# Gate and up products with stationary weights in runs of 16 and 32 of one width, also in the first chunk of three feed-forward parts

## The reference

```python
def swiglu(x, w_gate, w_up, w_down):
    return (jax.nn.silu(x @ w_gate) * (x @ w_up)) @ w_down
# each block:
h = h + 0.5 * swiglu(rms_norm(h, ffn1_norm), ffn1_w_gate, ffn1_w_up, ffn1_w_down)
h = h + mixer(rms_norm(h, mix_norm), ...)      # two attentions, gates, w_out
h = h + 0.5 * swiglu(rms_norm(h, ffn2_norm), ffn2_w_gate, ffn2_w_up, ffn2_w_down)
# the first block ends with one more rms_norm; the second takes its result as x
```

## Time and profile before

| | us |
|---|---|
| median of 3 runs | 1123.94 |
| lowest and highest | 1123.61, 1124.98 |
| span of the profiled execution | 1121.8 |
| PE busy in it | 1115.6 (99%) |
| DVE busy | 782.2 (70%) |
| ACT busy | 627.1 (56%) |

### The profile page before, as it was taken

How to read it: one execution, slowest core, us unless ns; L and a number is a source line. 1 busy time by engine, 2 the same in 40 slices (tenths; PEclk the granted TensorE clock), 3 DMA queues, 4 the chain that set the end, 5 groups by cost and what they waited for, 6 DMA issues and landing times.

```text
span 1121.8 us, 14828 instructions
## 1 busy us (share of the span) xinstructions
PE 1115.6 (99%) x5830; PEld 955.3 (85%) x5830; DVE 782.2 (70%) x1102; ACT 627.1 (56%) x837; POOL 57.8 (5%) x105
## 2 busy tenths in 40 slices
PE   9999999999999999999999999999999999999998
PEld 8888888888888888888888888888888888888887
DVE  6777755765887777775477777456998687777742
ACT  6555532677667456553355655337787864655530
POOL 1000000000000000000000000020353000000000
PEclk9999999999999999999999999999999999999999
DMA  9766565653454566655566655557643455556550
GB/s 319 246 189 190 187 244 190 207 168 131 161 187 160 178 216 189 188 188 188 188 207 188 188 188 188 188 165 255 212 151 116 148 164 176 186 188 189 191 183 37
DMA packets 142581, 208.02 MB, mean 185 GB/s; under 512 B 9296, under 2 KB 100584, under 8 KB 142512
## 3 DMA queue, kind: packets, MB, share of 16 engines
q1 hardware_dynamic: 139408, 198.07, 54.0%
q0 software_dynamic: 3088, 9.00, 2.3%
q10 hardware_dynamic: 16, 0.00, 0.0%
HBM read 205.98 MB, written 2.65 MB: 186 GB/s over the span
## 4 chain that ended last, share of the span: by engine, by line
PE 97%; DVE 1%; ACT 1%; DMA 0%; issue 0%; SPq 0%; DVEq 0%
PE banks L1796 26%; PE banks L1657 16%; PE banks L1659 16%; PE banks L1658 16%; PE banks L1794 14%; PE banks L1975 1%; PE banks L1729 1%; PE banks L1679 1%; PE banks L1949 1%; PE banks L1976 1%; PE banks L1900 1%; DMA raw<-in_ffn_w_gate 0%; PE banks L1933 0%; DVE w_lo L1122 0%; PE banks L1934 0%; PE banks L2040 0%
## 5 line engine op out<-in xcount | busy, mean ns | idle before, releaser
L1122 DVE TENSOR_TENSOR w_lo<-raw,w_hi 128x2048 fp32r<-128x2048 f32 x186 | 422.8, 2276 | 170.3 <-ACT w_hi L739 170.0
L739 ACT ACTIVATE w_hi<-raw 128x2048 fp32r<-128x2048 f32 x186 | 352.5, 1898 | 115.6 <-PE banks L1659 112.0
L1796 PE MATMUL banks<-xT,w_hi 128*128 128x512 f32 x1280 | 313.7, 392 | 0.0
L1796 PEld LDWEIGHTS banks<-xT,w_hi 128*128 128x128 f32 x1280 | 232.8, 189 | 43.2
L1657 PE MATMUL banks<-w_hi,xT 128*128 128x512 f32 (+1 forms) x464 | 183.2, 395 | 0.0
L1659 PE MATMUL banks<-w_hi,xT 128*128 128x512 f32 (+1 forms) x464 | 179.5, 387 | 0.0
L1658 PE MATMUL banks<-w_lo,xT 128*128 128x512 f32 (+1 forms) x464 | 179.2, 386 | 0.0
L1794 PEld LDWEIGHTS banks<-xT,w_lo 128*128 128x128 f32 x1280 | 169.8, 191 | 9.5
L1794 PE MATMUL banks<-xT,w_lo 128*128 128x256 f32 x1280 | 173.5, 283 | 0.0
L1657 PE MATMUL banks<-w_hi,hT_hi 128*128 128x512 f32 x352 | 137.4, 390 | 0.0
L1659 PE MATMUL banks<-w_hi,hT_lo 128*128 128x512 f32 x352 | 137.1, 389 | 0.0
(11 more groups left out here) (293 smaller groups left out, 917.8 us busy)
## 6 DMA issues: line engine op xcount, KB each, us to landing
raw<-in_ffn_w_gate SPq DMA_DIRECT2D x88, 512.0 KB, 4.0
raw<-in_ffn_w_up SPq DMA_DIRECT2D x88, 512.0 KB, 5.0
raw<-in_ffn_w_down SPq DMA_DIRECT2D x88, 512.0 KB, 4.3
raw<-in_w_in SPq DMA_DIRECT2D x76, 512.0 KB, 4.6
raw<-in_w_out SPq DMA_DIRECT2D x16, 512.0 KB, 4.1
raw<-in_w_branch_moba SPq DMA_DIRECT2D x4, 512.0 KB, 4.4
raw<-in_w_branch_sb SPq DMA_DIRECT2D x4, 512.0 KB, 5.6
raw<-in_w_branch_a SPq DMA_DIRECT2D x4, 512.0 KB, 3.8
```

The source lines that it names most:

```text
L739: act.activation(w_hi[u % SLOTS][:, 0:n], raw[u % RAWS][:, 0:n], ACT.Copy).then_inc(hi_done, 1)
L1122: dve.tensor_tensor(w_lo[r][:, 0:n], raw[r][:, 0:n], w_hi[u % SLOTS][:, 0:n], ALU.subtract).then_inc(lo_done, 1)
L1796: m = pe.matmul(bank[b + s], mh, xT[:, k].rearrange("p a s -> p (a s)"), start=k == 0, stop=k == KC - 1)
```

## The change

- In chunks 1 to 10 of all four parts the order becomes: 16 wide and 16 narrow products for hf = 0, then 16 narrow and 16 wide for hf = 1 (`pair_products`, `pair_chunk`, `pair_second`). With the neighbours that makes runs of 32. F0's turned hidden rows and the spread of 1/rms (`spread_rows`) now stand behind the first 16 wide products of chunk 1, before the narrow ones.
- In F1, F2 and F3 the first chunk becomes a pair chunk as well (`first_pairs`), narrow products first. The silu of tokens, its product and the four transposes are left in F0 alone (`first_silu`, `first_hidden`, `turn_hidden`). `spread_rows` stays, and waits for both sums of chunk 0.
- In these parts DVE's scaling of a gate is apart from the sum (`pair_scale`), and that of chunk 0 waits for `rows_copied`.
- Banks: even chunks use 0 to 3, odd ones 4 to 7, w_down sums in 4 to 7 (before 2 to 5), mixers turn x in 0 to 3 (before 0, 1, 6, 7), the spread rows are in bank 3.
- F2 takes its quarters in the order `Q_MIX` (before `Q_FFN`), and F1's w_down units go by it too (`down_quarters`).

```diff
+FIRST = {"F0": 1, "F1": 0, "F2": 0, "F3": 0}
...
         def quarters(ph):
-            return Q_MIX if ph in ("F0", "F1", "F3") else Q_FFN
+            return Q_MIX if ph[0] == "F" else Q_FFN
+
+        def down_quarters(ph):
+            return quarters(NEXT[ph]) if ph in NEXT else Q_FFN
...
-            return bank[2 + 2 * tt + n] if ph[0] == "F" else bank[2 * n + tt]
+            return bank[4 + 2 * tt + n] if ph[0] == "F" else bank[2 * n + tt]
...
-            return (2 if c % 2 else 0) + (2 * p if c % 2 else 6 * p)
+            return 4 * (c % 2) + 2 * p
...
-                silu(ph)
-                split_hi(u0 + 4)
-                hidden_hi(ph)
-                split_hi(u0 + 5)
-                rstd_rows_in(ph)
-                split_hi(u0 + 6)
-                for c in range(1, NCH):
+                if ph == "F0":
+                    act.wait_ge(rstd_done, 1)
+                    first_silu()
+                    split_hi(u0 + 4)
+                    first_hidden_hi()
+                    split_hi(u0 + 5)
+                    rstd_rows_in(ph)
+                    split_hi(u0 + 6)
+                else:
+                    split_hi(u0 + 4)
+                for c in range(FIRST[ph], NCH):
                     low(ph, c, 0)
-                    pair_gate(ph, c, 0)
+                    if c > 0:
+                        pair_gate(ph, c, 0)
                     low(ph, c, 1)
+                    if c == 0:
+                        rstd_rows_in(ph)
+                        pair_gate(ph, c, 0)
...
+            def pair_scale(ph, c, p):
+                n = pairs_before(ph, c) + p
+                if c == FIRST[ph]:
                     dve.wait_ge(rows_copied, FFN_OF[ph] + 1)
...
-                if ph != "F2":
+                if ph == "F0":
                     split_lo(u0 + 3)
-                hidden(ph)
-                split_lo(u0 + 4)
-                hidden_lo(ph)
-                split_lo(u0 + 5)
-                for c in range(1, NCH):
-                    pair_sum(ph, c, 0)
+                    first_hidden()
+                    split_lo(u0 + 4)
+                    first_hidden_lo()
+                    split_lo(u0 + 5)
+                else:
+                    pair_sum(ph, 0, 0)
+                    pair_sum(ph, 0, 1)
+                    if ph != "F2":
+                        split_lo(u0 + 3)
+                for c in range(FIRST[ph], NCH):
+                    if c:
+                        pair_sum(ph, c, 0)
+                    pair_scale(ph, c, 0)
                     pair_hidden(ph, c, 0)
                     split_lo(u0 + 4 + 2 * c)
                     pair_rest(ph, c, 0)
...
+            def pair_chunk(ph, c):
+
+                u = BASE[ph] + 2 * c
                 pe.wait_ge(lo_done, u + 1)
                 for p in range(2):
+                    pair_free(ph, c, p)
+                    pair_products(ph, c, 0, p, False)
+                if c == 1 and ph != "F2":
+                    spread_rows(ph)
+                for p in range(2):
+                    m = pair_products(ph, c, 0, p, True)
                 m.then_inc(unit_used, 1)
+                pair_second(ph, c)
+
+            def pair_second(ph, c):
+
+                pe.wait_ge(lo_done, BASE[ph] + 2 * c + 2)
+                for p in range(2):
+                    pair_products(ph, c, 1, p, True)
+                pair_products(ph, c, 1, 0, False).then_inc(pair_done, 1)
+                if c == 1 and ph == "F2":
+                    spread_rows(ph)
+                pair_products(ph, c, 1, 1, False).then_inc(unit_used, 1)
+
+            def first_pairs(ph):
+
+                u, x0 = BASE[ph], 4 * PREP_OF[ph]
+                turn_x(ph, 2 if ph != "F2" else 1)
+                if ph == "F2":
+                    turn_x(ph, 2)
+                pe.wait_ge(lo_done, u + 1)
+                pe.wait_ge(xT_hi_done, x0 + 2)
+                for p in range(2):
+                    if p:
+                        pe.wait_ge(gained, 4 * (3 if ph == "F2" else GAIN_OF[ph]) + 4)
+                    pair_products(ph, 0, 0, p, True)
+                turn_x(ph, 3)
+                pe.wait_ge(xT_lo_done, x0 + 2)
+                for p in range(2):
+                    m = pair_products(ph, 0, 0, p, False)
...
```

More of the change, by code:

```diff
@@ L1215, in scale_x, with first_hidden, first_hidden_lo @@
                 link(ins)
-            def hidden(ph):
+            def first_hidden():
                 for tt in range(TT):
-                    dve.wait_ge(silu_done, 2 * FFN_OF[ph] + tt + 1)
+                    dve.wait_ge(silu_done, tt + 1)
                     dve.tensor_tensor(hs[tt], bank[tt][:, CH:2 * CH], gsil[tt], ALU.mult).then_inc(h_done, 1)
-            def hidden_lo(ph):
-                dve.wait_ge(hT_hi_done, FFN_OF[ph] + 1)
-                dve.tensor_tensor(hT_lo[:, 0:2, :], bank[6].rearrange("p (k t) -> p k t", k=2),
+            def first_hidden_lo():
+                dve.wait_ge(hT_hi_done, 1)
+                dve.tensor_tensor(hT_lo[:, 0:2, :], bank[2].rearrange("p (k t) -> p k t", k=2),
                                   hT_hi[:, 0:2, :], ALU.subtract).then_inc(hT_lo_done, 1)
@@ L1750, in begin @@
                     return
-                turn_x(ph, EARLY[ph])
+                turn_x(ph, 1)
                 batch(0, 0)
-                for q in range(EARLY[ph] + 1, 4):
+                for q in range(2, 4):
                     turn_x(ph, q)
@@ L1757, in begin @@
                 batch(1, 1)
[L1759 to L1771, removed]
@@ L1773, in pair_chunk, with pair_products @@
-            def pair_chunk(ph, c, hf):
-                f = FFN_OF[ph]
-                u = BASE[ph] + 2 * c + hf
+            def pair_products(ph, c, hf, p, low):
+                u, b = BASE[ph] + 2 * c + hf, pair_banks(c, p)
+                for s in range(2):
+                    for k4 in range(4):
+                        k = 4 * hf + k4
+                        mh, ml = rows(u, NB, k4, s * CH + p * P, P)
+                        first = k == 0 and low == (c == 0)
+                        if low:
+                            m = pe.matmul(bank[b + s][:, 0:SEQ], ml, xT_hi[:, k, :], start=first, stop=False,
+                                          skip_group_check=c == 0)
+                        else:
+                            m = pe.matmul(bank[b + s], mh, xT[:, k].rearrange("p a s -> p (a s)"), start=first,
+                                          stop=k == KC - 1, skip_group_check=c == 0)
+                return m
@@ L1777, in pair_chunk, with pair_free @@
+            def pair_free(ph, c, p):
+                if c >= FIRST[ph] + 2:
+                    pe.wait_ge(pair_summed, pairs_before(ph, c - 2) + p + 1)
+                elif c == 2 and p == 0:
+                    pe.wait_ge(h_done, 2)
+                elif c == 2:
+                    pe.wait_ge(hT_lo_done, 1)
+                if c == 2 and p == 1:
+                    pe.wait_ge(rows_copied, FFN_OF[ph] + 1)
+            def pair_chunk(ph, c):
+                u = BASE[ph] + 2 * c
                 pe.wait_ge(lo_done, u + 1)
@@ L1778, in pair_chunk @@
                 for p in range(2):
[L1779 to L1797, removed]
@@ L1814, in turn_hidden, with spread_rows @@
-                pe.matmul(bank[7][:, 0:SEQ], ones, rstd_diag, start=True, stop=True).then_inc(rows_mm, 1)
+            def spread_rows(ph):
+                if ph == "F0":
+                    turn_hidden()
+                else:
+                    pe.wait_ge(pair_summed, PAIRS[ph] + 2)
+                pe.wait_ge(diag_done, 2 * FFN_OF[ph] + 2)
+                pe.matmul(bank[3][:, 0:SEQ], ones, rstd_diag, start=True, stop=True).then_inc(rows_mm, 1)
             def ffn(ph):
-                begin(ph, lambda tt, hf: first_chunk(ph, tt, hf))
+                if ph == "F0":
+                    begin(ph, None)
+                else:
+                    first_pairs(ph)
@@ L1818, in ffn @@
                 for c in range(1, NCH):
-                    pair_chunk(ph, c, 0)
-                    if c == 1 and ph != "F2":
-                        turn_hidden(ph)
-                    pair_chunk(ph, c, 1)
+                    pair_chunk(ph, c)
                 for d in range(NCH):
@@ L1826, in ffn @@
                     pe.wait_ge(lo_done, u + 1)
+                    if d < FIRST[ph]:
+                        pe.wait_ge(hT_lo_done, 1)
+                    else:
+                        pe.wait_ge(pair_lo, pairs_before(ph, d) + 2)
                     if d == 0:
[L1828 to L1832 removed]
+                        pe.wait_ge(pair_summed, pairs_before(ph, NCH - 1))
+                    for q, (tt, n) in enumerate(down_quarters(ph)):
                         if d == NCH - 1 and q == 3 and ph in NEXT:
```

89 lines of the change are left out of this document (42 added, 47 removed).

## The result

The changed kernel takes 1129.65 us (median of 4 runs, 1128.12 to 1130.16) against 1124.01 us before: a ratio of 1.0049, 95% interval 1.0037 to 1.0061. It is slower, by 5.6 us where 4.2 were forecast. The profiled execution spans 1127.8 us (before 1121.8).

What follows compares the result with a forecast made beforehand. PE's stream of products was taken as the bound. Waits of +6.5 us and work of -2.3 gave +4.2, a profiled 1126.0 and a median of 1128.2 us; the 8-in-10 range was 1126.3 to 1130.7.

Steps and rivals of the forecast that it cites:

- PE's stream is the bound: Whole kernel: PE is busy 1115.6 of 1121.8 us, so work removed is gained and uncovered waits are lost in full.
- Part 1, runs, -1.6: Chunks 1 to 10: two fewer changes of width per chunk at 0.02 us, over 40 chunks, save 1.6 us.
- the prediction's rival: Chunks 1 to 10: changes of width are free, so 1.6 us less is gained, 1129.8 us; chance 0.08.
- Part 2, first chunk and transposes, +0.6 and -1.3: First chunk of F1, F2, F3: 64 products instead of 48 cost 0.6 us; dropped hidden-row transposes save 1.3.
- F0, +1.8: F0, chunk 1: transposes, now ahead of 16 narrow products, wait for DVE's hidden products; 1.8 us lost.
- Seams, +0.7 and +1.6: Starts of F1 and F3: waits for the last quarter's gain, 0.7 us; F2: waits for xT_hi and gain, 1.6.
- F2's chunk 2, +2.4: F2: chunk 2's first unit is split only after the 1/rms chain, so PE waits; 2.4 us lost.
- that rival: F2: PE's clock falls after the 2.4 us wait, costing about 2 us more, 1130.2 us; chance 0.08.
- One sign of being wrong: Listed signs: no idle PE at F2's chunk 2, period 11.15 or under 11.0, or F2 stretches with granted clock under 1.
- The start as evidence for the clock: Kernel start: five 512-column products take 2.50 us, some 0.53 each where 0.23 is usual, read as low pace.
- The thin cover behind it: F2, after chunk 2's wait: next unit split 0.4 us before PE asks, no further wait; further waits up to 1.5 us, chance 0.05.

Runs made afterwards that it cites:

- the runs alone: Kernel before, only the product order of chunks 1 to 10 changed to 16 wide, 16 narrow, 16 narrow, 16 wide: 1122.31 us, ratio 0.9987.
- all waits covered: Changed kernel with F0's transposes later, F2's second quarter turned earlier, gain waits moved or dropped, chunk 2's units in F2 split before the 1/rms wait: 1121.61 us.

## Why the prediction was right, and where its size was off

- **PE's stream is the bound.** Right: F0's wait and the two of F2's seam came back in the time in full when they were taken away, F2's wait at chunk 2 less what a new wait took, and a kernel without any of them is faster than before by the saved work.
- **Part 1, runs, -1.6.** Right: period 11.154 to 11.114, and 1.4 by the runs alone. By the rule of the Trainium skill (TensorE: Matmul & The Clock Gate, "Step-by-step: what each phase is for") that the next weights load while the current product runs, the prediction's rival had 0 here; the measurement decides against 0. It doesn't show what a change of width spends its time on. The prediction took 0.107 us for a load although the trace of before has rows for it, of 0.191 us on average, longer than the 0.12 us from one narrow product to the next. The loads overlap one another (1280 x 0.191 is 244 us, in 169.8 us of busy time; the row has the count, busy us, mean ns and idle us):

```profile
L1794 PEld LDWEIGHTS banks<-xT,w_lo 128*128 128x128 f32 x1280 | 169.8, 191 | 9.5
```

- **Part 2, first chunk and transposes, +0.6 and -1.3.** Right as a sum: -0.7 between the kernel with all waits covered and that with the runs alone. They differ in this and in what goes with it (banks, the order of the quarters, the order of ACT's and DVE's queues), and have the same waits. The two terms were not measured one by one.
- **F0, +1.8.** Right: 1.7 by the rows, 1.7 to 1.8 by the experiment.
- **Seams, +0.7 and +1.6.** F2's was right (1.4 to 1.6). Those of F1 and F3 were not taken away one by one; they are in the 6.6 of all waits. In F1's trace the third quarter's transposes to chunk 1 are 12.40 us against 11.84 in the earlier trace rows, 0.56 more, forecast 0.19 + 0.36; the wait is in the first 16 narrow products, which take 2.37 us instead of some 2.0 (1.91, and 0.09 behind transposes). F3's was not read:

```profile
382.40 0.60 PE L1703 MATMUL banks<-const,xg 128*128 128x128 f32 x4
382.76 2.54 PE L1792 MATMUL banks<-xT,w_lo 128*128 128x256 f32 x16
385.13 0.60 PE L1703 MATMUL banks<-const,xg 128*128 128x128 f32 x4
...
394.80 3.82 PE L1795 MATMUL banks<-xT,w_hi 128*128 128x512 f32 x16
```

- **F2's chunk 2, +2.4.** The wait was right in its place and its length. Its price was not complete: the clock falls behind it in 5 of 9 runs, at 1.6 us. The step of the prediction that failed is the weight given to that rival (0.08, and nothing in the sum) and not its size (2 us). No ground was given for so small a weight: the prediction says itself that waits of up to 1.1 us don't show what a longer one does. The median, 1129.65, is of the rival's group (1130.2 forecast, 1129.8 measured); the forecast's own 1128.2 is the other group's. One sign of being wrong thus came true, a stretch of F2 with a granted clock under 1, and that the median came within 1.5 us of the forecast is in part luck: how many runs of a few have the fall decides it.
- **The start as evidence for the clock.** The prediction read the slow products at the start, 0.53 us each, as a low clock. The granted clock in that stretch was 1.00, so they are no evidence for it, and what slows them stays open:

```profile
1.00:5.00 4.00, 3.94 (x9) 2.50 (x9) 0.31 (x3) 1.01 (x1) 0.00 (x0) 1.00 0.73 207
```

- **The thin cover behind it.** "0.4 us before PE asks for it" held in the changed kernel at full clock: chunk 2's second unit is split by 600.16 and asked for at 600.64. But the two experiments that moved the first unit's split showed this second unit late by 0.3 us.

## What to carry to other kernels

Before the stream of a bound engine is reordered, note for each of its waits what was queued ahead of it as cover: here 16 narrow products ahead of four transposes, and a split ahead of a wait for 1/rms, were worth more than the reordering gained. Where TensorE is the bound, a single idle stretch can cost more than its length, as the one of 2.2 us did in half of the runs here by bringing the lower clock; price it with and without. And move a split or any other long instruction only after following what then stands behind it.

## What the runs showed of the hardware

- A change of width and back costs some 0.02 us: two of them fewer per chunk took its period from 11.154 to 11.114 us. The rows are too coarse to say on which side it falls (16 wide products take 3.66 us, twice 8 take 3.68). Longer runs gain nothing more: the second 16 of a run of 32 wide products take 0.23 us each, as before.
- The granted clock fell behind a single wait of 2.2 us in 13 of 25 runs of three kernels that have it (5 of 9, 4 of 11, 4 of 5), and behind one of 4.0 us in 4 of 4. It never fell behind waits of 1.3 to 1.6 us (5 runs with two of them, 11 with one). The place of the fall is seen in four profiled executions (three with the wait of 2.2 us, one with 4.0); in the others the fall is taken from the mean clock (0.998 or less) and the time. The Trainium skill (TensorE: Matmul & The Clock Gate, "Why this matters for your kernels") tells to avoid idle gaps of TensorE between bursts of products, and the trace agrees; but the gap that it names is longer than the 2.2 us that were enough here in half of the runs.
- At the lower level, 16 wide products behind the wait took 5.21 us instead of 3.77. The low stretch was 3.4 us, and 1.6 us of the run were lost.
